# Routing gates of a product-key expert layer: a one-hot matmul stage replaced by a gate table in DRAM

## What is computed

```python
    v1, i1 = lax.top_k(s1, PEER_TOPK)
    v2, i2 = lax.top_k(s2, PEER_TOPK)
    cand = (v1[..., :, None] + v2[..., None, :])      # 16 x 16 sums
    cand_idx = (i1[..., :, None] * PEER_NKEYS + i2[..., None, :])
    top_s, pos = lax.top_k(cand, PEER_TOPK)
    expert_idx = jnp.take_along_axis(cand_idx, pos, axis=-1)
    gate = jax.nn.softmax(top_s, axis=-1)
    ...
        u = w_down[ib]
        act = jax.nn.gelu(jnp.einsum("td,thkd->thk", xb, u), approximate=False) * gb
        v = w_up[ib]
        return jnp.einsum("thk,thkd->td", act, v)
```

## Time and profile before

| | us |
|---|---|
| device time, median of 3 runs | 2239.06 (2238.25 to 2239.7) |
| span of the profiled execution, first to last instruction | 2235.5 |
| device time less span | 3.6 |

### The profile page before, as it was taken

How to read it: one execution, slowest core, us unless ns; L and a number is a source line. 1 busy time by engine, 2 the same in 40 slices (tenths; PEclk the granted TensorE clock), 3 DMA queues, 4 the chain that set the end, 5 groups by cost and what they waited for, 6 DMA issues and landing times.

```text
span 2235.5 us, 42971 instructions
## 1 busy us (share of the span) xinstructions
PE 2164.0 (97%) x15644; PEld 2022.3 (90%) x15644; DVE 1609.0 (72%) x2891; ACT 1191.2 (53%) x1723; POOL 322.3 (14%) x226
## 2 busy tenths in 40 slices
PE   7988999999998899999999999999999999989999
PEld 6987899999997788888899999789999999869999
DVE  6796569999968855555578765767666766887774
ACT  5455357777777755555544444544344434764443
POOL 4786100000005400000011010010000001241000
PEclk9999999999999999999999999999999999999999
DMA  4432465656554165556665565235565556414656
GB/s 162 143 112 82 140 197 185 188 183 184 187 179 134 54 188 188 187 185 189 186 204 174 175 191 166 67 95 175 172 188 179 173 175 191 122 36 138 183 187 188
DMA packets 108088, 359.57 MB, mean 161 GB/s; under 512 B 13104, under 2 KB 21680, under 8 KB 107872
## 3 DMA queue, kind: packets, MB, share of 16 engines
q1 hardware_dynamic: 105904, 354.04, 50.6%
q10 hardware_dynamic: 2096, 4.36, 0.6%
HBM read 356.22 MB, written 6.46 MB: 162 GB/s over the span
## 4 chain that ended last, share of the span: by engine, by line
PE 83%; DVE 10%; ACT 3%; POOL 2%; issue 2%; DMA 1%; SPq 0%; ACTq 0%; DVEq 0%; POOLq 0%
PE ps L557 19%; PE ps L559 19%; PE ps L558 19%; PE ps L862 16%; PE ps L794 3%; DVE ring_lo L446 2%; DVE hot_keys L1683 2%; DVE big L1692 2%; POOL ring_lo L446 1%; ACT w_hi L440 1%; POOL slot_t L2586 1%; POOL big L2605 0%; PE ps L1195 0%; PE ps L826 0%; DVE big L2011 0%
## 5 line engine op out<-in xcount | busy, mean ns | idle before, releaser
L446 DVE TENSOR_TENSOR ring_lo<-ring,w_hi 128x1024 fp32r<-128x1024 f32 x600 | 749.5, 1250 | 219.4 <-ACT w_hi L440 215.5
L557 PE MATMUL ps<-hw_hi,w_hi 128*128 128x272 f32 (+1 forms) x3104 | 890.2, 287 | 13.6 <-DVE ring_lo L446 3.6
L440 ACT ACTIVATE w_hi<-ring 128x1024 fp32r<-128x1024 f32 x640 | 676.0, 1057 | 407.7 <-DMA ring<-in_ffn_in_dram 138.2
L559 PE MATMUL ps<-hw_hi,ring_lo 128*128 128x272 f32 (+1 forms) x3104 | 887.1, 286 | 0.0
L558 PE MATMUL ps<-hw_lo,w_hi 128*128 128x272 f32 (+1 forms) x3104 | 885.1, 285 | 0.0
L557 PEld LDWEIGHTS ps<-hw_hi,w_hi 128*128 128x128 f32 x3104 | 586.9, 189 | 21.8 <-issue 10.8
L559 PEld LDWEIGHTS ps<-hw_hi,ring_lo 128*128 128x128 f32 x3104 | 587.4, 189 | 0.0
L558 PEld LDWEIGHTS ps<-hw_lo,w_hi 128*128 128x128 f32 x3104 | 585.6, 189 | 0.1
L862 PE MATMUL ps<-w_hi,hid_parts 128*128 128x512 f32 x1024 | 281.3, 396 | 2.3 <-DVE hid_parts L1711 2.3
L862 PEld LDWEIGHTS ps<-w_hi,hid_parts 128*128 128x128 f32 x1024 | 193.0, 189 | 49.5 <-issue 2.5
L557 PE MATMUL ps<-gated_hi,w_hi 128*128 128x272 f32 (+1 forms) x704 | 201.3, 286 | 0.0
(11 more groups left out here) (437 smaller groups left out, 2522.9 us busy)
## 6 DMA issues: line engine op xcount, KB each, us to landing
ring<-in_ffn_in_dram SPq DMA_DIRECT2D x176, 512.0 KB, 3.5
ring<-in_down_dram SPq DMA_DIRECT2D x128, 512.0 KB, 3.5
ring<-in_up_dram SPq DMA_DIRECT2D x128, 512.0 KB, 3.5
ring<-in_ffn_out_dram SPq DMA_DIRECT2D x96, 512.0 KB, 3.6
ring<-in_a_in_dram SPq DMA_DIRECT2D x24, 512.0 KB, 3.5
ring<-in_xbc_dram SPq DMA_DIRECT2D x16, 512.0 KB, 3.7
ring<-in_conf_dram SPq DMA_DIRECT2D x16, 512.0 KB, 3.5
ring<-in_mix_out_dram SPq DMA_DIRECT2D x16, 512.0 KB, 3.5
```

Source lines behind the costliest of these rows:

```text
L440: nc.scalar.activation(w_hi[:, u % RING, :], ring[:, u % RING, :], ACT.Copy).then_inc(hi_done, 1)
L446: eng.tensor_tensor(ring_lo[:, u % RING, :], ring[:, u % RING, :], w_hi[:, u % RING, :].bitcast(F32), ALU.subtract).then_inc(split_done, 1)
L557: nc.tensor.matmul(bank_out, w_hi[:, b, w], hi(k0 + k), start=start and k == 0, stop=False)
L559: last = nc.tensor.matmul(bank_out, ring_lo[:, b, w], hi(k0 + k), start=False, stop=stop and k == m - 1)
```

## The change

The one-hot stage is gone. A table `gates` of 16,384 x 256 floats (16.8 MB) in DRAM takes its place: the row of an expert is its gate for each token. There are five parts.

1. **Clearing.** 64 transfers of 256 KB write zeros from a blank tile into `gates` (`clear_pair`). SP issues one behind each weight load from xbc unit 4 up to query unit 11.
2. **Routing.** The key numbers are multiplied by their strides and summed in one lookup of 512 elements, which gives the place of (expert, token) in the table directly (`slot`). There are 25 results and 6.25 splits per pair of head and token tile, and the softmax is done pair by pair: ACT's Exp stands at fixed units (`EXP_AT`), 6.25 units apart, and `finish_gate` of a pair is done at the end of the pair that follows. PE's transposes and DVE's copies of them fall away. ACT's down pass is written out instead of looped.
3. **Scattering.** POOL issues 256 indirect transfers, 16 behind each pair. One transfer adds 128 gates (one per token, 4 bytes each) into 128 places of the table. It waits for `gate_ready` of its pair and, so that no two additions of a token to one expert meet, for the transfers of the same tokens' previous head.
4. **Loading.** SP waits for all 256, behind the last load of the down pass; then it issues the first 4 tiles of gates and behind them the first 4 weight units of the up pass. Later it issues one tile (128 KB) behind each weight unit. POOL multiplies the tile into `hid` (`gate_hidden`), and `hidden_high` waits for that.
5. **Moved.** The up pass accumulates in PSUM banks 4 to 7 instead of 0 to 3. `h` stays where it is: the spill and the reload go. The `bias_rows` transfer is issued as the down pass begins instead of as the one-hot stage begins.

```diff
@@ SP @@
+            def clear_pair(n):
+                dst = gate_pairs[n] if isinstance(n, int) else gate_pairs[bass.ds(n, 1)].rearrange("a p e t -> (a p) e t")
+                sp.dma_start(dst, bc(blank, 1, 2)).then_inc(blanked, 16)
...
-            stream("xbc", 1)
-            for name in ("conf", "z"):
-                stream(name)
+            sp.wait_ge(blank_made, 1)
+            stream("xbc", 1, None, -RING)
+            stream("conf", 0, None, 12)
+            stream("z", 0, None, 28)
...
             stream("down")
+            for t in range(2):
+                sp.wait_ge(scattered[t], 16 * PEER_HEADS * TOPK)
+            for s in range(RING):
+                load_gate(s, s)
             stream("up", 0, 1)
-            sp.wait_ge(gates_mm, SEQ // 8)
-            sp.wait_ge(h_spilled, 16)
-            sp.dma_start(h[:, :, META:T], h_spill).then_inc(h_back, 16)
...
-            stream("up", 1)
+            with sp.Fori(1, UNITS["up"] // RING) as it:
+                for s in range(RING):
+                    sp.wait_ge(unit_done, it * RING + (UNIT0["up"] + s - RING + 1))
+                    load_unit("up", it * RING + s, s)
+                    sp.wait_ge(gated_hid, it * RING + (s - RING + 1))
+                    load_gate(it * RING + s, s)
@@ PE @@
-            for n in range(SEQ // 8):
-                b = n % 2
-                pe.wait_ge(hot_dve, n + 1)
-                pe.wait_ge(hot_act, n + 1)
...
@@ DVE @@
+                step(V_.tensor_tensor(pick, bc(pos_f.rearrange("p h k -> p k h"), 3, TOPK),
+                                      bc(bc(C("iota", TOPK), 1, 2), 1, TOPK), ALU.is_equal))
+                step(V_.tensor_tensor(pick, pick, bc(top_f, 1, TOPK), ALU.mult))
+                step(V_.tensor_reduce(place, pick.rearrange("p k h j -> p k (h j)"), AX, ALU.add))
+                step(V_.tensor_scalar(slot[:, t, span], place, C("token", 2)[:, t:t + 1], None, ALU.add))
+                if g:
+                    finish_gate(g - 1)
@@ ACT @@
+            act.dma_start(bias_rows.rearrange("h (q r) -> h q r", r=REL), bc(u_table, 1, P)).then_inc(u_spread, 16)
...
+                act.wait_ge(gate_in, g + 1)
+                v = gate[:, t, hd * TOPK:(hd + 1) * TOPK]
+                A_(v, v, ACT.Exp, bias=top_0[:, g:g + 1], accum_out=gate_sum[:, g:g + 1]).then_inc(gate_exp, 1)
...
+                act.wait_ge(gated_hid, it * 4 + (c + 1))
                 A_(hid_parts[:, c % PARTS, :], at(hid, it * 4 + c), ACT.Copy).then_inc(hid_hi_done, 1)
@@ POOL @@
+            for g in range(2 * PEER_HEADS):
+                hd, t = g // 2, g % 2
+                pool.wait_ge(gate_ready, g + 1)
+                if hd:
+                    pool.wait_ge(scattered[t], 16 * TOPK * hd)
+                for k in range(hd * TOPK, (hd + 1) * TOPK):
+                    nc.gpsimd.indirect_dma_start(gates, bass.IndirectOffsetOnAxis(slot[:, t, k:k + 1], 0), gate[:, t, k:k + 1], None,
+                                                 compute_op=ALU.add).then_inc(scattered[t], 16)
+
+            def gate_hidden(it, s):
+                i = it * RING + s
+                pool.wait_ge(gate_loaded[s], it * 16 + 16)
+                nc.gpsimd.tensor_tensor(at(hid, i), at(hid, i), gate_tile[:, s, :], ALU.mult).then_inc(gated_hid, 1)
```

More of the change, by code:

```diff
@@ L829, in _ @@
             pe.wait_ge(xn_ready, KD)
[L830 to L853 removed]
+            loop_8("down", normed(META), SEQ)
             def up_unit(it, s, start, stop):
@@ L1695, in _ @@
-            dve.wait_ge(unit_done, UNIT0["up"])
-            high_digits(0)
-            one_hots(0)
-            one_hots(1)
-            high_digits(1)
-            for n in range(SEQ // 8):
-                gate_hidden(n)
-                if n in (8, 16):
-                    dve.wait_ge(hot_dve, n)
-                    high_digits(n // 8 + 1)
-                if n + 2 < SEQ // 8:
-                    one_hots(n + 2)
+            finish_gate(2 * PEER_HEADS - 1)
+            while ahead[0] < UNITS["down"] + 2:
+                low("down", ahead[0])
+                ahead[0] += 1
```

248 lines of the change are left out of this document (81 added, 167 removed).

## The result

The changed kernel took **2371.7 us** (median of 4 runs, 2368.9 to 2377.5) against 2238.7 us before (4 runs beside it, 2238.3 to 2239.7): a ratio of 1.060, 95% interval 1.058 to 1.061. It is 133 us slower. I had forecast 2161 us and a range up to 2340; both were wrong.

The account below looks back on a forecast made before the run. PE's matmul stream was taken to bound the kernel, with the one-hot stage DVE-bound. 79.4 + 1.6 - 1 - 1 - 1 = 78 us off the 2235.5 us span, plus 3.6 outside it, gave 2161 us; range 2152 to 2340.

Parts of the forecast that it names:

- The stage goes, 79.4 us: Between down and up pass: the 80.9 us one-hot stage leaves the chain, a 1.5 us seam remains; gain 79.4 us.
- The down pass, DVE level with PE: In the down pass: DVE needs 17.5 us a pair against PE's 17.7; 4.6 us saved less 3 gains 1.6 us.
- `bias_rows`, 1 us of 0 to 5: In the down pass: the 4.2 MB transfer now runs with the weight stream; cost 1 us, of 0 to 5.
- the ring still covers them: In the down pass: loads of 5.2 instead of 3.5 us, issued three units (8.5 us) ahead, still arrive in time.
- Clearing, 1 us: Before the down pass: writing 16.8 MB of zeros behind weight loads costs 1 us, of 0 to 8.
- The scatter, c = 1.1 us: POOL spends c on each of 256 transfers; at 1.1 us they end about 634 us, hidden up to 1.25, cost 0.
- C: Rival in the scatter: POOL's transfers and DVE's work exclude each other, or c is simply large; 2245 us and up, chance 0.33.
- D: Rival in the down pass: additions in DRAM crowd out weight loads, so PE waits; 2187 us or slower, chance 0.07.
- The up pass, 1 us: In the up pass: gate tiles and POOL's product fit within a unit's 2.77 us; cost 1 us, of 0 to 30.
- c below 1.25: Main case: POOL's time per transfer leaves the scatter hidden and DVE is level with PE; 2161 us, chance 0.40.

## Why the prediction was wrong

Point by point, in its own order.

**The stage goes, 79.4 us: right.** The chain no longer has it, and with the scatter out of the way the seam is 1.4 us for the 1.5 forecast.

**The down pass, DVE level with PE: right.** PE waits for `ring_lo` once in the pass, and that one is the late load; 128 units and all friction are 363.7 us with `bias_rows` away, against 362.8 + 3. DVE's splits wait for ACT only 0.2 us in 360 to 540 us (8.6 before), so it has no time to spare, but it isn't late.

**`bias_rows`, 1 us of 0 to 5: mis-sized.** It costs 5 to 7 us in the down pass: the first 480 matmuls take 61.7 to 64.0 us in the nine traces with the transfer there and 56.9 in all four without. In the kernel before 4.6 us of it are left in the time. The step that failed is "the ring still covers them". I spread 19 us of transfer over 41 us of pass and loads over 5.2 us each; in the trace it takes all it can get at once, 347 GB/s in 322 to 335 us, and the load of the fifth unit takes 9.1 us. With rounding and split it is 11.6 us from its issue until PE starts, where my count gave it 8.5; PE waits 3.2. And I had not counted what follows a stall: ten microseconds at a granted clock of 0.74 on the average (a matmul takes 0.21 us, so it is the lower of the two levels, 1.2 GHz, for part of them, and then 2.4 again), in which 67 matmuls are done where 85 fit. That is another 2 us behind the 3.2 us of waiting. No run has the transfer in the middle of a pass.

**Clearing, 1 us: about right, not isolated.** The down pass begins 1.0 us later than before. No run takes the clearing away; among the kernels here that clear the whole table it begins between 318.7 and 324.0 us, in the two that clear nothing at 318.7 and 318.3, so the price lies between 0 and 6 us.

**The scatter, c = 1.1 us: this is the step that failed.** Measured c is 1.54 + 0.30 = 1.84 us with DVE idle and (445.4 + 78.8) / 256 = 2.05 over the whole, inside my bounds of 0.18 to 2.42 and far from the value taken. The rest of that step holds: with 2.05 its own formula gives 352 + 525 + 2.5 = 879, 204 us past 675, and 2161 + 204 = 2365 us; measured 2371.7. Two misses of it nearly cancel: the first transfer starts at 363.3 and not at 352 (6.3 us of that are the stall by `bias_rows`; with it away the first starts at 357.0), and without the hole PE would have begun the up pass at 691 and not at 683. So the time follows from c alone. The value was chosen by likeness to a fill of 1,024 columns, which has nothing in common with a transfer but an engine. Three things are in the price of which no row of before showed any: about 1.25 us for the instruction, 2 ns and more for each row that is added, and 0.30 us of gap.

**The rivals.** C had the place right (POOL late, PE waiting for it) and the mechanism half. POOL and DVE do exclude each other, and the measured excess of 51 us is below the 16 x 9.3 = 149 us that I gave it, since the subtraction holds a transfer only if that begins inside it. C decided from 1.56 us on; the transfer alone, with no DVE beside it, is past that. The Trainium skill ("SBUF — State Buffer", Who interferes with whom) says that two-input operations do not hold POOL's descriptor writing up, and copies, casts and one-scalar operations in the two-port mode do. The same section says that a DVE instruction with two SBUF inputs contends with a POOL instruction that reads SBUF; I had left that out, though a transfer here reads its places from SBUF. The traces agree with both halves: the two-input subtraction held transfers 0.13 us behind their start, 50.2 us on 85 of them, and no later; the one-input multiplication held them later too, 7.3 us on 38. That the first point is the reading and the second the writing is my guess; no run here shows it. D is out: the DMA share reached 0.76 to 0.79 against 0.73 forecast, and the pass runs at the same pace with 16, 128 or 256 transfers. A packet takes twice my 22 ns (4.4% of 16 engines' 2367 us over 36864 packets is 45 ns), but an added row is one packet and not three.

**The up pass, 1 us: right, by two terms that cancel.** Without the hole it takes 357.6 us, 2.2 less than before; with it 359.6. Most of the difference, 1.6 us, lies in the first 120 matmuls, where TensorE comes out of 200 idle microseconds at a granted clock of 0.80 on the average over its first 11 us.

**The chances.** All but one term of the sum were within some 6 microseconds, and none of that mattered. I gave 0.40 to c below 1.25, though the two bounds lay 2.24 us apart and nothing in the trace lay near. Spread evenly between them, c is above 1.25 with 0.52, above 1.56 with 0.38 and above 1.95, where my range ended, with 0.21. The range had to reach that last part.

## What to carry to other kernels

Where a change rests on hundreds of instructions of a kind that the trace doesn't have, work out first the price per instruction at which the gain is gone (here 1.56 us), and treat a value chosen by likeness as unknown over its whole bounds. An indirect transfer from POOL is paid by the instruction, hardly by the row, so what counts is how many there are: the part of them that fits beside other work is free, and a mix that sends only that part (128 of 256) kept half of the stage's time. A big transfer that was free in an idle stage has to be placed anew when that stage goes: at the head of a pass 4.2 MB cost 5 to 7 us at the down pass and 9 to 11 us at the up pass, though the first four units of either came in time.

## What the runs showed of the hardware

- An indirect transfer of 128 rows of 4 bytes keeps POOL for 1.54 us when it adds (144 packets) and 0.96 us when it writes (32 packets), with 0.30 us of gap behind it; 64 and 16 added rows take 1.41 and 1.28 us (80 and 32 packets).
- A transfer that begins inside DVE's subtraction or multiplication over 1,024 columns of SBUF is held nearly until that ends (0.46 us of 0.59, 0.74 of 0.87, 0.32 of 0.45). One that has begun is not disturbed by the two-input subtraction, but the one-input multiplication holds it again at about 1.46 us (38 transfers, 7.3 us).
- 4-byte additions in DRAM, 80 transfers of 128 rows in 180 us of the down pass in the place of 10, took 16 points of the DMA engines' share (0.62 to 0.78) and cost the weight stream nothing: 306.9 us from the 481st matmul to the end of the pass in both kernels.
- TensorE's granted clock was 0.50, the level of 1.2 GHz, while PE stood idle for 196 us, and 0.80 on the average over the first 11 us of work behind that; behind a stall of 3 us it was 0.74 on the average over 10 us of unbroken work, and 1.00 (2.4 GHz) after both.
